# A sample state update moved from the delta-rule recurrence (TensorE, VectorE, ScalarE, GpSimd) to GpSimd alone, later in the kernel

## What is computed

```python
def step(s, xs):                              # gated_delta_recurrent, one step
    q_t, k_t, v_t, g_t, b_t = xs
    s = s * jnp.exp(g_t)[..., None, None]
    u = b_t[..., None] * (v_t - jnp.einsum('bhk,bhkv->bhv', k_t, s))
    s = s + jnp.einsum('bhk,bhv->bhkv', k_t, u)
    return s, jnp.einsum('bhk,bhkv->bhv', q_t, s)
```

## Time and profile before

| What | Value |
|---|---|
| three runs | 1497.41, 1498.08, 1503.62 us (median 1498.08) |
| profiled execution: span from first to last instruction | 1498.6 us (no other time of it is given) |
| TensorE busy | 1477.9 us (99%) |
| VectorE, ScalarE, GpSimd busy | 531.3, 348.2, 109.4 us |
| mean granted TensorE clock | 0.997 |
| recurrence, `a_out`, `wi` (from the timeline) | about 190 to 281, 261 to 308, 308 to 437 us |

### The profile page before, as it was taken

The page is one execution under the profiler, slowest core; times in us unless marked ns, Lnnn a source line. Parts: engine busy times, 40 slices in busy tenths (PEclk is TensorE's granted clock), DMA queues, the critical chain, the costliest instruction groups (busy, mean ns, idle before and its releaser), DMA issues.

```text
span 1498.6 us, 33271 instructions
## 1 busy us (share of the span) xinstructions
PE 1477.9 (99%) x14663; PEld 1025.3 (68%) x14663; DVE 531.3 (35%) x879; ACT 348.2 (23%) x603; POOL 109.4 (7%) x185
## 2 busy tenths in 40 slices
PE   8999999999999999999999999999999999999997
PEld 8999888899999989555555554554554554555543
DVE  6767876766665684301101101101111111011113
ACT  6556557354444443200000000000000000000001
POOL 0011147200000000100000000000000000000010
PEclk9999999999999999999999999999999999999999
DMA  6778623755545757999999999999999999999992
GB/s 256 298 276 290 227 84 112 260 187 174 192 153 180 289 230 277 415 401 419 401 418 419 402 419 419 402 420 419 401 419 419 400 420 419 398 420 418 418 417 108
DMA packets 78053, 490.70 MB, mean 327 GB/s; under 512 B 9304, under 2 KB 9560, under 8 KB 53216
## 3 DMA queue, kind: packets, MB, share of 16 engines
q1 hardware_dynamic: 70000, 460.41, 77.4%
q0 software_dynamic: 7920, 28.25, 5.4%
HBM read 464.71 MB, written 23.92 MB: 326 GB/s over the span
## 4 chain that ended last, share of the span: by engine, by line
PE 92%; DVE 3%; DMA 2%; ACT 2%; issue 1%; SPq 0%; DVEq 0%; ACTq 0%
PE PP L2662 39%; PE PP L1991 25%; PE PP L2672 19%; ACT dhi L404 1%; DVE dlo L410 1%; DMA ring<-in_mkv 1%; DMA ring<-in_a_out 1%; PE PP L2109 1%; PE PP L2221 1%; PE PP L2093 1%; PE PP L2545 0%; PE PP L2085 0%; PE PP L2071 0%; PE PP L2322 0%; DMA ring<-in_wi 0%
## 5 line engine op out<-in xcount | busy, mean ns | idle before, releaser
L2662 PE MATMUL PP<-ring,gen 128*32 128x448 f32 x6144 | 580.4, 539 | 1.7 <-DVE gen L1845 1.2
L2662 PEld LDWEIGHTS PP<-ring,gen 128*32 128x32 f32 x6144 | 317.6, 110 | 263.1 <-issue 261.3
L2672 PE MATMUL PP<-ring,gen 128*32 128x512 f32 x2688 | 291.5, 592 | 0.1
L2672 PEld LDWEIGHTS PP<-ring,gen 128*32 128x32 f32 x2688 | 138.6, 110 | 149.7 <-issue 149.5
L1991 PE MATMUL PP<-uh,dhi 128*128 128x264 f32 x736 | 214.4, 291 | 1.3 <-DVE dlo L410 1.1
L1929 DVE TENSOR_TENSOR gen<-ubuf,PP 128x448 f32<-128x448 f32 x48 | 26.9, 616 | 518.2 <-PE PP L2662 518.2
L1991 PE MATMUL PP<-ul,dhi 128*128 128x264 f32 x736 | 209.4, 285 | 0.0
L1991 PE MATMUL PP<-uh,dlo 128*128 128x264 f32 x736 | 209.2, 284 | 0.0
L1152 ACT ACTIVATE ubuf<-PP 128x448 f32<-128x448 f32 x48 | 22.6, 544 | 781.7 <-PE PP L2662 781.7
L410 DVE TENSOR_TENSOR dlo<-ring,dhi 128x2048 fp32r<-128x2048 f32 (+2 forms) x77 | 161.4, 2096 | 85.2 <-ACT dhi L404 84.9
L404 ACT ACTIVATE dhi<-ring 128x2048 fp32r<-128x2048 f32 (+2 forms) x77 | 135.2, 1756 | 92.4 <-PE PP L1991 69.4
(11 more groups left out here) (495 smaller groups left out, 1423.9 us busy)
## 6 DMA issues: line engine op xcount, KB each, us to landing
ring<-in_w_up SPq DMA_DIRECT2D x256, 896.0 KB, 19.1
ring<-in_w_down SPq DMA_DIRECT2D x112, 1024.0 KB, 19.4
ring<-in_wi SPq DMA_DIRECT2D x22, 1024.0 KB, 4.9
ring<-in_a_in SPq DMA_DIRECT2D x18, 1024.0 KB, 7.4
ring<-in_wo SPq DMA_DIRECT2D x16, 704.0 KB, 4.1
slot_rows<-ring POOLq DMA_DIRECT2D x25, 384.0 KB, 5.1
ring<-in_mkv SPq DMA_DIRECT2D x8, 1024.0 KB, 5.0
ring<-in_kc SPq DMA_DIRECT2D x8, 1024.0 KB, 9.9
```

What stands on the lines that cost most here:

```text
L2662: mm = pe.matmul(bank((c // KD % 2) * SG + g)[SL * q:SL * (q + 1), 0:FQ], xs[:, at_:at_ + SL], w[:, q * FQ:(q + 1) * FQ], start=(k == 0), ...
L2672: return pe.matmul(out[SL * quarter:SL * (quarter + 1), :], hT[:, at_:at_ + SL], w[:, k * D + h * 512:k * D + (h + 1) * 512], start=(j == ...
```

## The change

The outer products, the eight sums, the multiplications by the decay on ScalarE and GpSimd and the block rows go from the recurrence. The `u` rows are written to a DRAM tensor `sample_u`. After the store of `S` and the load of `poolbuf`, GpSimd's queue loads each quarter of the state again into `s_part` (two buffers in the space of `cat`, `mk`, `mv`), and the matching 16 rows of `u` spread over all 128 partitions into `u_all`. It then makes three operations of 128x2048 on each quarter and stores it. The first high parts of `wi` no longer wait for stores; the store waits move to the start of the normed rows after `wo`.

```diff
-            faded(0)
-            pool.wait_ge(s("sd_row"), 3)
-            pool.wait_ge(s("sd_cat"), 1)
...
-            sample_values(0)
-            sample_values(1)
-            faded(1)
-            sample_values(2)
-            sample_values(3)
-            faded(4)
-            faded(6)
...
-            sent(0)
-            faded(7)
-            for i in range(1, 4):
-                sent(i)
+            pool.wait_ge(s("sd_row"), 2)
+            for g in range(4):
+                pool.dma_start(sample_u.rearrange("(i g) c -> g i c", g=4)[g], urow[32 * g:32 * g + 16]).then_inc(s("u_sent"), 16)
             pool.wait_ge(s("S_done"), 2)
             pool.dma_start(outs["S"], Sb).then_inc(s("kv_S_stored"), 16)
             pool.wait_ge(s("kv_S_stored"), 80)
             pool.memset(diag_b, 0.0).then_inc(s("diag_zero"), 1)
             pool.dma_start(poolbuf, ins["poolbuf"]).then_inc(s("poolbuf_loaded"), 16)
...
+            def load_state(x):
+                pool.dma_start(s_part[x % 2], ins["state"][x]).then_inc(s(f"s_part_loaded{x % 2}"), 16)
+
+            def load_u(x):
+                pool.dma_start(u_all, sample_u[16 * x:16 * (x + 1)].rearrange("(a n) c -> a (n c)", a=1).to_broadcast([P, DCH]))\
+                    .then_inc(s("u_loaded"), 16)
+
+            pool.wait_ge(s("u_sent"), 64)
+            pool.wait_ge(s("m_lo"), CAT_READ)
+            load_u(0)
+            load_state(0)
+            load_state(1)
+            for x in range(4):
+                part = s_part[x % 2]
+                pool.wait_ge(s("u_loaded"), 16 * (x + 1))
+                pool.tensor_tensor(by_state(u_all), by_state(u_all), per_state(kcol, x), ALU.mult).then_inc(s("state_new"), 1)
+                pool.wait_ge(s(f"s_part_loaded{x % 2}"), 16 * (x // 2 + 1))
+                pool.tensor_tensor(by_state(part), by_state(part), per_state(sgb, x), ALU.mult).then_inc(s("state_new"), 1)
+                pool.wait_ge(s("state_new"), 3 * x + 2)
+                pool.tensor_tensor(part, part, u_all, ALU.add).then_inc(s("state_new"), 1)
+                pool.wait_ge(s("state_new"), 3 * x + 3)
+                pool.dma_start(outs["state"][x], part).then_inc(s("state_stored"), 16)
+                if x < 3:
+                    load_u(x + 1)
+                if x < 2:
+                    pool.wait_ge(s("state_stored"), 16 * (x + 1))
+                    load_state(x + 2)
```

More of the change, by code:

```diff
@@ L73 @@
 LV = 5
-FADED_EARLY = [0, 1, 4, 6, 7]
-FADED_ACT = [2, 3, 5]
+CAT_READ = 3 * KD + 5
 HALF = H * 32
@@ L287, in build @@
         qku = cut(gen, DS + 384, 64)
-        krow = cut(gen, DS + 448, 128)
         kqrow = cut(gen, DS + 704, 128)
-        own16 = cut(gen, DS + 1728, 16)
-        kpad, upad = (cut(ring, arena + 6400 + 128 * i, 128) for i in range(2))
-        assert 4096 + 1744 <= 5840 and 6400 + 256 <= CT * PRE
+        upad = cut(ring, arena + 6400, 128)
+        assert 4096 + 832 <= 5840 and 6400 + 128 <= CT * PRE
         urow = cut(gen, DS + 576, 128)
-        ublk = [cut(gen, DS + 704 + 512 * i, 512) for i in range(2)] + [cut(ring, arena + CT * (PRE + ACTW) - 768 - 512 * i, 512) for i in range(2)]
+        u_all = cut(gen, 0, DCH)
+        s_part = [cut(gen, DCH * (i + 1), DCH) for i in range(2)]
+        kcol = cut(gen, DS + 448, DBH)
+        assert 4096 + 832 <= 5240
+        sample_u = nc.dram_tensor("sample_u", (DBH, P), F32).ap()
         sil = [cut(gen, SC + 2640 + 264 * i, 264) for i in range(2)]
@@ L594, in _ @@
             store(outs["conv"], convio)
[L596 to L602, removed]
             pool.wait_ge(s("coef_dif"), 1)
@@ L926, in half @@
                 return b[:, g * 512:(g + 1) * 512]
[L928 to L934, removed]
             def key_quads(c):
@@ L1061, in residual_norm @@
                     a.wait_ge(s("h_new"), (i - 2) * KD + t + 1)
+                    if i == 3 and t == 0:
+                        a.wait_ge(s("state_stored"), 64)
                     a.activation(uh[i - 1][:, t * T:(t + 1) * T], h[:, t, :], ACT.Copy, scale=gains[:, b + t:b + t + 1])\
@@ L2313, in half_z @@
                 mm.then_inc(s("dl_z"), 1)
[L2315 to L2322, removed]
             pe.wait_ge(s("conv_silu"), 24)
@@ L2389, in _ @@
             pe.wait_ge(s("ain_out"), 36)
-            pe.matmul(bank(7)[:, 0:64], ones[:, :], kqd, start=True, stop=True)
-            pe.transpose(bank(7)[:, P:2 * P], kpad, ident).then_inc(s("sd_rows"), 1)
+            pe.matmul(bank(7)[:, 0:64], ones[:, :], kqd, start=True, stop=True).then_inc(s("sd_rows"), 1)
             step_z(4, 0)
@@ L2420, in _ @@
             half_y(1)
-            outer(0)
             for x in range(H):
@@ L2436, in _ @@
             head_sums(0, bank(4), 0, P)
-            outer(1)
             pe.wait_ge(s("dl_vt"), 3)
@@ L2480, in _ @@
             mm.then_inc(s("dl_ds"), 1)
-            outer(5)
             a_out_tile(0, XH, len(order), lambda i: base_a + need[XH + i]).then_inc(s("aout_mm"), 1)
-            outer(6)
             for t in range(1, KD):
-                if t == 2:
-                    outer(7)
                 if t == 4:
-                    pe.wait_ge(s("state_new"), 16)
+                    pe.wait_ge(s("sd_row"), 2)
+                    pe.wait_ge(s("sd_cat"), 1)
                 if t == 6:
```

53 lines of the change are left out of this document (7 added, 46 removed).

## The result

The changed kernel takes 1530.07 us (median of four runs, 1528.52 to 1534.51) beside 1498.96 us for the kernel before, measured next to it: the ratio is 1.0201, with a 95% interval of 1.0182 to 1.0220. The forecast was 1513 us with a range to 1524. The profiled execution has a span of 1528.5 us, 29.9 more than before.

The account below looks back on a forecast made before the run. TensorE, busy for 99% of the span, was taken to bound the kernel. The recurrence's -5.4 us, +13.5 in `wi` and +7 in `a_out` sum to +15.1, giving 1513 us, range 1497 to 1524.

Parts of the forecast that it names:

- The recurrence: Removing the outer products there takes work off TensorE and gains 5.4 us, with bounds of 3 and 9.6.
- Nothing by themselves: In the recurrence, `outer(3)` and `outer(4)` lie in waits for inverse roots and VectorE's multiply, so removing them alone gains nothing.
- GpSimd's operations: Twelve beside `a_out` and `wi`: 3.9 us for two of three, 4.6 for the third, from about 285 to 400.
- The way into SBUF: Beside `a_out` and `wi`, VectorE or GpSimd holds it for a whole operation; VectorE waits up to 4.15 us.
- The round: One GpSimd operation, then VectorE's three without a gap: 1.5 us lost per operation in `wi`, 2.4 in `a_out`.
- rival 3: In `wi`, GpSimd gets in after every single VectorE operation: 3.3 us each, about 40 for twelve, 1533 us; chance 0.05.
- Rival 4: Transfers decide if `wi` loads pass 7.4 us: some 1 to 3 us per burst, 1504 us; chance 0.04.
- Rivals 1 and 2: GpSimd costs VectorE next to nothing, likeliest 1494.5 us (0.16); or the recurrence gives 9.6 and the port nothing, 1489 (0.05).
- What would show it: `a_out` tile 2 near 274.5 us, lines 411 and 1636 at 4 to 6, TensorE waits of 1 to 2.5.
- All later stages carry the shift: Later stages are bound by TensorE and its loads, so the whole shift is carried to the end.

Follow-up runs that it names:

- e4b: Changed kernel with each of GpSimd's twelve operations replaced by two fills of 128x2048, which read nothing; 1509.83 us.
- e5: Changed kernel with each of GpSimd's twelve operations cut into sixteen pieces of 128x128; 1510.22 us.
- e3: Changed kernel with GpSimd's twelve operations in a row, without loads, spreads and stores of the state; 1529.01 us.
- e2: Changed kernel without any of the new part: no operations, loads, spreads or stores of the state; 1493.11 us.
- e9: Changed kernel with all transfers, but GpSimd's three operations on the last quarter only; 1514.5 us.
- e1: Changed kernel without GpSimd's twelve operations, all loads, spreads and stores kept; 1502.26 us.
- e6: Changed kernel with the decay moved to ScalarE and the update to VectorE, in gaps of `wi` tiles, GpSimd only issuing transfers; 1502.39 us.
- e7: e6 with a second buffer for `u` and each transfer waiting for another `wi` tile; 1498.12 us.
- e8: e7 with two unused products of 128x512 put on TensorE ahead of its two waits in the recurrence; 1495.33 us, ratio 0.9972.

## Why the prediction was wrong in size

- **The recurrence**, -5.4 us: at `a_out` tile 2 the kernel after is 7.2 us ahead, 2.8 of which lie ahead of the first outer product, where it lacks the pause of 1.96 us at 205.59. The change doesn't touch that place, so these 2.8 are luck. The 4.4 us left are the sum less what it didn't see, 3.52 for 2.05 us of line 2428; the terms were not separated. "Nothing by themselves" for `outer(3)` and `outer(4)` was right as to the waits and missed that they kept TensorE at work.
- **GpSimd's operations**: 3.61 us with the spread operand and 4.56 with two full ones, for 3.7 to 3.9 and 4.6. The first began at 280.7 us, for 284 to 289; twelve were done at 360.8 us, not at 400. So six lay beside `a_out` and six beside `wi`, not three and nine; at the prediction's own prices that is 23.4 us for 20.5, a small part of the miss.
- **The way into SBUF**: right. The Trainium skill, SBUF — State Buffer, section "Who interferes with whom", has the second of two such instructions wait until the first is through; line 1624's 3.84 us for 0.42 agrees, and `e4b`'s unchanged 2292 ns says that GpSimd must be reading. The 7.66 us of `e5` go beyond it: there VectorE waited through sixteen instructions, not one.
- **The round, the step that failed**: "After that all three are ready and go without a gap, as in the earlier trace rows". In after and `e3` GpSimd gets in behind each single operation of VectorE, even where VectorE's next is ready. The round is then all three of GpSimd's with all three of VectorE's, 13.5 us, 3.0 us an operation (`e3` less `e2`; 2.8 in after's table), not 1.5 in `wi` and 2.4 in `a_out`. That is rival 3, which had 3.3 and about 40 us, 1533 us, and a chance of 0.05 on the strength of one member of 2915 ns in the earlier trace rows. The prediction's bound for this rival, 50 us, and its price, 40, don't agree; 35.9 were measured. Turns explain neither the 2915 ns nor the 7660 of `e5`; what lets one engine go twice stays open.
- **The clock**, a term that the sum lacked: 1.5 us in the recurrence, 2.5 in after's tile 5, 2.0 in `e9`.
- **Rival 4**, the transfers: its price was right (9.2 us for 10), and so was its condition, a load of more than 7.4 us: 9.8 at the longest in `e1`, 9.2 in after. It decides in `e1` and `e6`, where the stalls are gone. In after one late load stands ahead of the second burst (ScalarE waited 6.0 us for it, VectorE 4.9 for ScalarE), so a part of the cost there can be the transfers'; `e3` comes to the same total without any. **Rivals 1 and 2** fell with the lengths of lines 411, 1636 and 1624.
- **What would show it**: lines 411 and 1636 at 4 to 6 us came true nearly (up to 6.58 and 3.82), and so did the place. TensorE began `a_out` tile 2 at about 272.7 us for 274.5: the 2.8 us that are luck, less the 1.0 by which the recurrence fell short. TensorE's waits of up to 8.0 us, eight of them, in place of 1 to 2.5 us in some ten tiles, were the sign of rival 3.
- **All later stages carry the shift**: it held to the last but one tile of `wo` (+26.8). Another 3.1 us came after, 1.4 of them in the last tile of `wo`, and no run tells whether that is more than chance.

## What to carry to other kernels

Ask of work that is moved to an engine off the path not how busy that engine is but how long one of its instructions is against the spare of the engine it shares its reads with: VectorE's 65% of idle time did not help, because its short operations waited 2 to 4 us each for a long one. Work for gaps belongs on the engine that has the gap, in pieces that fit it, with its transfers one to a tile. And count filler: an outer product in a wait costs nothing, and without it TensorE's clock fell in nine kernels of ten.

## What the runs showed of the hardware

- VectorE with two inputs in SBUF and GpSimd with two inputs in SBUF took turns, one instruction each, throughout after and `e3`: 4.59, 3.83, 4.76 us on VectorE for 1.75, 0.49, 0.43, beside 3.61, 5.11, 4.61 on GpSimd (`e3`). Once each an engine stood through more than one: GpSimd through two of VectorE's (2915 ns for 597), VectorE through sixteen of GpSimd's of 0.42 us (7.66 us for 1.75, `e5`). A fill on GpSimd stops nothing: line 411 keeps its 2292 and 1758 ns (`e4b`). The time spent waiting counts as busy in the profile (6.58 us for 2.29, line 411 in after).
- Behind waits of 1.7 and 1.5 us, with a product of 0.7 us between them, the granted clock fell to the lower level in nine kernels (421 ns for 275 a matmul in the median in `e7`) and not in a tenth (`e4b`). With two unused products of 512 columns in the waits it stayed at full speed (`e8`).
- A megabyte of weights that lands in 4.9 us took 8.8 to 9.6 us at worst with GpSimd's queue loading and storing megabytes beside it (`e6`).
